# Block one: second tile of the fourth modulation block multiplied behind the query's first half, its rows turned inside the query's second half

## The reference

```python
sc = jax.nn.silu(c)
mx = (sc @ w_mod[l] + b_mod[l])[:, None, :]          # 1024 x 6144: "modulation"
sh1, sc1, g1, sh2, sc2, g2 = jnp.split(mx, 6, axis=-1)
...
spec_x = hyena_spectrum(n_lat, hy_f_w1[l], ...)       # sin(freq * (feats @ w1 + b1)), again with w2
hx = modulate(rms_norm(x, norm1_g[l]), sh1, sc1)      # x * (1 + sc1) + sh1
# in mixer_sublayer: p = h @ w_in; q = p[..., 0:512] (the query), then k, v, hyena, fourier, gates
...
x = x + g2 * expert_choice_moe(h2, w_router, w_gate, w_up, w_down)   # 16 experts, 384 MB of weights
```

## Time and profile before

| | us |
|---|---|
| median of 3 runs | 2284.73 |
| lowest and highest | 2281.32, 2289.18 |
| the profiled execution's own time | 2282.55 |
| span of the profile | 2281.2 |
| PE busy | 1927.4 (84%) |
| DVE busy | 985.9 (43%) |
| ACT busy | 670.2 (29%) |

### The profile page before, as it was taken

How to read it: one execution, slowest core, us unless ns; L and a number is a source line. 1 busy time by engine, 2 the same in 40 slices (tenths; PEclk the granted TensorE clock), 3 DMA queues, 4 the chain that set the end, 5 groups by cost and what they waited for, 6 DMA issues and landing times.

```text
span 2281.2 us, 28991 instructions
## 1 busy us (share of the span) xinstructions
PE 1927.4 (84%) x12332; PEld 1340.5 (59%) x12332; DVE 985.9 (43%) x1235; ACT 670.2 (29%) x817; POOL 66.7 (3%) x144
## 2 busy tenths in 40 slices
PE   7899998666556665566689999999999999999998
PEld 4777952111111111111138998779998999788997
DVE  4855741000000000000006657876567666876656
ACT  4433420000000000000005434554445444455444
POOL 0000000000000000000001001010000000100000
PEclk9999999887788777888799999999999999999999
DMA  9256799999999999999996554245544555325552
GB/s 388 103 217 235 307 403 430 431 431 430 431 430 432 432 432 430 431 432 430 430 426 248 195 203 162 95 157 185 194 168 174 187 199 177 147 97 177 200 190 85
DMA packets 53489, 647.44 MB, mean 284 GB/s; under 512 B 5936, under 2 KB 6448, under 8 KB 10096
## 3 DMA queue, kind: packets, MB, share of 16 engines
q1 hardware_dynamic: 53360, 645.59, 71.0%
HBM read 644.52 MB, written 1.05 MB: 283 GB/s over the span
## 4 chain that ended last, share of the span: by engine, by line
PE 58%; DMA 31%; DVE 6%; ACT 2%; issue 1%; POOL 1%; SPq 0%; DVEq 0%; ACTq 0%; POOLq 0%
DMA wide_a<-in_experts 28%; PE PS L504 14%; PE PS L506 14%; PE PS L505 14%; PE PS L968 5%; PE PS L1003 3%; DMA ring<-in_fg 2%; DVE low L1905 1%; DMA ahead<-in_wmod 1%; PE PS L946 1%; PE PS L522 1%; PE PS L657 1%; DVE PS L1930 1%; PE PS L872 1%; PE PS L1280 1%
## 5 line engine op out<-in xcount | busy, mean ns | idle before, releaser
L1905 DVE TENSOR_TENSOR low<-ring,WH 128x2048 fp32r<-128x2048 f32 (+1 forms) x163 | 372.1, 2283 | 180.6 <-ACT WH L2294 178.0
L504 PE MATMUL PS<-XH,WH 128*128 128x256 f32 x1408 | 396.9, 282 | 3.6 <-DVE XL L1937 3.4
L505 PE MATMUL PS<-XL,WH 128*128 128x256 f32 x1408 | 395.2, 281 | 0.0
L506 PE MATMUL PS<-XH,low 128*128 128x256 f32 x1408 | 393.1, 279 | 0.0
L2294 ACT ACTIVATE WH<-ring 128x2048 fp32r<-128x2048 f32 (+1 forms) x164 | 313.1, 1909 | 24.0 <-DMA ring<-in_fg 16.0
L504 PEld LDWEIGHTS PS<-XH,WH 128*128 128x128 f32 x1408 | 264.5, 188 | 7.1 <-issue 5.4
L506 PEld LDWEIGHTS PS<-XH,low 128*128 128x128 f32 x1408 | 267.4, 190 | 0.0
L505 PEld LDWEIGHTS PS<-XL,WH 128*128 128x128 f32 x1408 | 264.6, 188 | 1.4
L1887 DVE TENSOR_TENSOR T1S<-T1S,PS 128x512 f32<-128x512 f32 x16 | 11.0, 688 | 539.2 <-PE PS L968 539.2
L968 PE MATMUL PS<-ring,big 128*32 128x512 f32 x968 | 137.2, 713 | 57.7 <-DMA ring<-in_experts 57.7
L2570 ACT ACTIVATE T1S<-PS 128x512 f32<-128x512 f32 x16 | 9.6, 597 | 545.2 <-PE PS L968 545.2
(11 more groups left out here) (446 smaller groups left out, 2740.3 us busy)
## 6 DMA issues: line engine op xcount, KB each, us to landing
wide_b<-in_experts SPq DMA_DIRECT2D x29, 4096.0 KB, 23.7
ring<-in_experts SPq DMA_DIRECT2D x29, 4096.0 KB, 24.1
wide_a<-in_experts SPq DMA_DIRECT2D x29, 4096.0 KB, 23.7
ring<-in_fg SPq DMA_DIRECT2D x44, 1024.0 KB, 5.0
ring<-in_fu SPq DMA_DIRECT2D x44, 1024.0 KB, 5.0
ring<-in_fd SPq DMA_DIRECT2D x44, 1024.0 KB, 4.9
ahead<-in_wmod SPq DMA_DIRECT2D x18, 1024.0 KB, 8.5
ring<-in_wgt SPq DMA_DIRECT2D x12, 1024.0 KB, 4.8
```

The source lines that it names most:

```text
L504: t.matmul(o, l[0], r[0], start=start, stop=False, skip_group_check=True)
L505: t.matmul(o, l[0], r[1], start=False, stop=False, skip_group_check=True)
L506: return t.matmul(o, l[1], r[0], start=False, stop=stop, skip_group_check=True)
L1905: own(v.tensor_tensor(low[:, w.slot.index, 0:size], w.flat, WH[:, w.slot.index, 0:size].bitcast(f32), ALU.subtract).then_inc(*c.wl.up()), ...
```

## The change

Only PE's order changes. Both tiles of block 3 were multiplied together, then came `filter_in(1)`, `q_half(0, 0)`, the turn of block 3, and `q_half(1, 0)`. Now only the first tile is multiplied ahead of `q_half(0, 0)`; the second stands behind it; the turn stands in the middle of `q_half(1, 0)`; and `filter_in(1)` stands behind `q_half(1, 0)`.

```diff
-            def q_half(m, h):
+            def q_half(m, h, ks=range(4)):
                 P.wait_ge(c.xtv, 2 * h + 2)
-                if h == 0:
+                if h == 0 and 0 in ks:
                     take(m)
-                for k in range(4 * h, 4 * h + 4):
+                for k in [4 * h + k for k in ks]:
...
-                i.then_inc(*c.q.up())
+                if 3 in ks:
+                    i.then_inc(*c.q.up())
...
             mod_turn(1)
             mod_turn(2)
-            mod_products(3)
+            mod_products(3, (0,))
+
+
+            q_half(0, 0)
+            mod_products(3, (1,))
+            q_half(1, 0, (0, 1))
+            mod_turn(3)
+            q_half(1, 0, (2, 3))
             filter_in(1)
-
-
-            q_half(0, 0)
-            mod_turn(3)
-            q_half(1, 0)
             filter_out(0)
             q_half(0, 1)
```

## The result

| | before | changed |
|---|---|---|
| median, us | 2285.79 (9 runs) | 2290.66 (9 runs) |
| lowest and highest | 2281.32, 2289.18 | 2289.21, 2291.91 |
| profiled execution's own time | 2282.55 | 2290.38 |
| span | 2281.2 | 2289.1 |

The ratio is 1.0029, 95% interval 1.002 to 1.0037: slower by 6.6 us, between 4.6 and 8.5. (The ratio isn't the quotient of the two medians, which lie 4.87 us apart, 1.0021.) The forecast was 2291.8 us in a range of 2286.5 to 2296.

A forecast was written before the change was run, and what follows sets the result against it. Block one's compute was taken to feed DMA, so any shift there delays the full DMA stage. A 5.5 us shift plus 2.1 us of low clock gave +7.6 us, forecast 2291.8 us, range 2286.5 to 2296.

The forecast's parts named there:

- likeliest case: Main forecast: DVE chain delayed 5.5 us plus 2.1 us of low clock, +7.6 us; range +5.5 to +9.5, chance 0.54.
- What bounds the kernel: Block one's compute feeds DMA before 280 us; no place between 42 and 380 us swallows a shift of some microseconds.
- Steps (a) to (c): PE's start: first tile ends at 31.13 us, q_half(0, 0) starts at about 31.38, 2.7 us earlier, and ends at 35.25.
- I keep 33.57: PE's granted clock still rises from 0.50 to 1.00 at 33.57 us, as before the change.
- two clock costs: Rival: low clock lasts through q_half(0, 0), +1.4 us, and the later fall costs 2.9; +9.8 us, 2294.5 us, chance 0.12.
- Steps (d) to (g): PE: second tile at full clock to 36.3 us (0.9 won), query slices and turn, second query part done at 40.0.
- Step (h): DVE gets the late filter's product and starts the second sine's argument at 40.65 us instead of 34.25, 6.4 us late.
- Step (i): DVE's argument takes 2.85 us, so block 3's bias starts at 43.52 us instead of 38.02, a shift of 5.5 us.
- Step (k): PE idles about 6 us ahead of 46.57 us and resumes at a low clock; 2.1 us lost, between 0 and 2.9.
- Sum: Whole kernel: +5.5 us shift plus 2.1 us low clock makes +7.6 us, forecast 2291.8 us.

The follow-up runs named there:

- experiment 2: The kernel before with only the filter's product moved, behind the query's first half; 2291.03 us, ratio 1.0031 against the kernel before.
- experiment 4: Changed kernel with DVE's filter argument behind bias, scaling and low part, PE's filter_out(0) and filter_out(1) one query part later; 2289.15 us, ratio 1.0023.
- experiment 1: The changed kernel with the filter's product put back ahead of the query, behind block 3's first tile; 2285.64 us, ratio 1.0008 against the kernel before.
- experiment 6: The changed kernel with 25 identity products in PE's idle time behind the filter's product; 2290.97 us, ratio 1.0027 against the kernel before.
- experiment 3: The changed kernel with 20 identity products in PE's idle time behind the filter's product; 2291.30 us, ratio 1.0032 against the kernel before.
- experiment 11: The changed kernel with 25 identity products in PE's idle time, measured again; 2290.59 us, ratio 1.0033 against the kernel before.
- experiment 8: The kernel before measured and profiled again, no edit; 2284.50 us, ratio 1.0003.
- experiment 7: Kernel before with filter's product ahead of block 3, turn inside q_half(0, 0), 4 and 6 identity products in PE's earlier waits; 2283.18 us, ratio 0.9997.
- experiment 9: experiment 7 with 7 more identity products in PE's wait at 77 us; 2282.89 us, ratio 0.9994 against the kernel before.

## Why the prediction was right

The forecast was +7.6 us, which it put at 2291.8 us; the measured medians are 2290.66, and 2291.64 in the second measurement. The mechanism was forecast and is shown. That the sum came so close has some luck in it: the shift at the query's end was 8.8 us, 1.2 more than the sum, of which 0.7 us were gone when block two's first weights were asked for (8.14) and another 0.3 us at the end (7.83). The difference of the first medians, 4.87 us, lies below the likeliest case's own range of 5.5 to 9.5. The base moved as well: the forecast stood on 2284.73 us, the median of three runs, and nine gave 2285.79.

- **What bounds the kernel**: right. The shift went from `in_wfn` to the experts unchanged (8.82 to 8.83 us), so nothing swallowed it there. Behind it, up to block two's first weights, 0.7 us went in these two profiles, which the forecast had at nothing.
- **Steps (a) to (c)**: right in kind, and near in number by two errors that cancel in part. The query started at 30.5 us, earlier than 31.4: the tile had ended at 29.8, and the low part that the query waited for was ready 0.86 us earlier in that execution (30.46 instead of 31.32). "I keep 33.57" for the clock did not hold. The low clock lasted 6.8 us as before, but it began at 28.85 us instead of 26.75 and ended at 35.7, so that nearly all of `q_half(0, 0)` ran at 1.2 GHz and ended at 35.8, not at 35.25. That is the first half of the rival *two clock costs* (start plus 1.81 x 2.89 = 35.7), made up for by the early start. The products at 1.2 GHz started 0.43 us apart, which no row had shown; the factor of 1.81 from the modulation tile was slightly small against 0.43 / 0.23 = 1.86. The Trainium skill's page "TensorE: Matmul & The Clock Gate", section on the gate, gives some 427 ns for 512 columns at 1.2 GHz. This trace agrees: ten distances from 31.10 to 35.37 us make 0.427 us each.
- **Steps (d) to (g)**: the tile took 1.06 us (forecast 1.0), the bank was copied out in time, PE reached the filter's product at 40.7 (forecast 40.0).
- **Step (h)**, the one on which all hangs: shown. DVE waited until 41.47 (forecast 40.65). Experiment 2 gets the whole cost, within the noise, from this edit alone; experiment 4 takes the delay away at the bias without touching the late product; experiment 1 takes the cost away by the product's place.
- **Step (i)**: 5.5 us was 0.8 too small, it is 6.33 us: 0.7 because PE reached the filter's product later, mostly by the later clock, and 0.1 because 0.75 us and not 0.65 passed between that product and DVE's start.
- **Step (k)**: 2.1 us forecast, 2.5 us in the profile (8.83 less 6.33); experiment 6, which holds the clock, gives 2.5 us as well. That it reaches the program's end in full is not shown: experiments 3, 6 and 11 measured no faster than the change beyond noise. In both profiles with the gap closed (6 and 11) the clock fell near 85 us, in both of the changed kernel it did not; whether the one makes the other more likely stays open, since experiment 4 had a fall at both places and the first profile of the kernel before at neither.
- **Sum**: by the first profiles the change costs 7.8 us, by the medians 4.9 and 6.9 us, by the ratios 6.6 and 8.2 us. What the profiles have too much is in the base: the first profile of before had its low clocks short, and experiment 8 stood 2.06 us behind it at 128 us and 4.81 us at 334 us. The changed kernel's runs lie within 2.7 us of each other in the first measurement, those of before within 7.9 us.

## What to carry to other kernels

Before moving a small product to fill another engine's idle time, find who reads it and what is queued behind that reader: here 0.6 us of PE's work, moved by 7 us, held five steps of DVE that the critical chain needed, and the turn waited 5 us to be picked up. Move the reader with the product, or neither. And when a change is worth some microseconds, take the profile of the unchanged kernel twice: here two of them differed by 4.8 us at one and the same instruction.

## What the runs showed of the hardware

Up to block two the granted clock was the largest source of spread that the traces show. The same program had it at 0.50 for 6.8 and for 10.2 us at the start; not at all and for 3.4 us near 80 us; for 3.4 and 6.8 us behind the router (10.2 us in experiment 11). Three places cost 1.05, 1.0 and 2.75 us in one execution against another, which makes up the whole 4.81 us.

It fell without a long idle time. Ahead of the fall at 81.1 us of experiment 8 stood a wait of 2.08 us. At the start it fell 0.5 us behind a wait of 2.01 us in the changed kernel (at 28.85 us), but ahead of that wait in the kernel before (at 26.75 us), and in experiments 7 and 9 (at 28.4 and 28.1 us) with no idle time of PE in the 11 us ahead of it. In all of them the turns' 16 tiny products (128x2, some 2 us) end within 2.6 us of the fall. Whether these are the cause is not shown.

Identity products of 128 columns went with a clock of 1.00 through the 6 us in which PE had nothing else to do (experiments 6 and 11), where it fell in both profiles of the changed kernel and in experiment 2; but in experiments 7 and 9 it fell 0.1 us into a run of them.
